# Two transformer blocks on one core: seven of eight rows of four norms squared and summed one stage earlier, and the mixers' first weights asked for first

## What is computed

```python
def rms_norm(x, g):
    xf = x.astype(jnp.float32)
    y = xf * lax.rsqrt(jnp.mean(xf * xf, axis=-1, keepdims=True) + EPS)
    return (y * g.astype(jnp.float32)).astype(x.dtype)
...
        h = h + 0.5 * swiglu(rms_norm(h, g_ffn1[i]), w_ffn1_gate[i], w_ffn1_up[i], w_ffn1_down[i])
        u = rms_norm(h, g_mix[i]) @ w_in[i]
...
        h = h + jnp.concatenate([o_mla, o_diff], axis=-1) @ w_out[i]
        h = h + 0.5 * swiglu(rms_norm(h, g_ffn2[i]), w_ffn2_gate[i], w_ffn2_up[i], w_ffn2_down[i])
        gate = jax.nn.sigmoid(rms_norm(h, g_ple_in[i]) @ w_ple_gate[i] + b_ple_gate[i])
        h = h + gate * rms_norm(p[i] @ w_ple_proj[i], g_ple_out[i])
...
        h = h + mixer(rmsnorm(h, norm_mix_g[l]), w_in[l], ...)
```

## Time and profile before

| | |
|---|---|
| median of 3 runs | 2608.38 us (2603.45 to 2608.44) |
| the profiled execution | 2611.73 us |
| its span in the trace | 2609.8 us |
| TensorE busy | 2296.4 us, 88% |
| VectorE busy | 961.0 us, 37% |
| ScalarE busy | 451.7 us, 17% |
| GpSimd busy | 50.8 us, 2% |
| granted TensorE clock, mean | 0.94 |

### The profile page before, as it was taken

One profiled execution on the slowest core, in us unless ns is written; L12 is line 12 of the kernel. 1 busy time (PEld: TensorE's weight loads), 2 busy tenths in 40 slices (PEclk: granted clock), 3 DMA queues, 4 the chain that ended last, 5 costly groups with the idle time before them and its releaser, 6 DMA issues.

```text
span 2609.8 us, 26212 instructions
## 1 busy us (share of the span) xinstructions
PE 2296.4 (88%) x10107; PEld 1560.8 (60%) x10107; DVE 961.0 (37%) x1961; ACT 451.7 (17%) x851; POOL 50.8 (2%) x76
## 2 busy tenths in 40 slices
PE   7999999989989999999989997779999587777783
PEld 5888887336644888887558774456785332222231
DVE  5454433133743455434310207876651300000003
ACT  2000001253351001000210014432113000000001
POOL 0000000000000000000000000000000000000001
PEclk9999999999999999999989987789999699989997
DMA  3232222111005323231132210000332589999996
GB/s 128 65 97 87 87 88 91 46 35 33 1 9 181 118 79 97 75 119 57 41 90 69 65 41 1 1 9 1 97 113 92 226 372 429 428 430 429 429 415 246
DMA packets 172359, 359.92 MB, mean 138 GB/s; under 512 B 15665, under 2 KB 144305, under 8 KB 155874
## 3 DMA queue, kind: packets, MB, share of 16 engines
q1 hardware_dynamic: 163744, 326.89, 33.8%
q0 software_dynamic: 5600, 21.10, 2.1%
q10 hardware_dynamic: 2914, 10.56, 1.0%
HBM read 337.49 MB, written 21.04 MB: 137 GB/s over the span
## 4 chain that ended last, share of the span: by engine, by line
PE 27%; DMA 12%; DVE 5%; issue 4%; DVEq 2%; ACT 1%; POOLq 1%; SPq 1%; POOL 0%; ACTq 0%
DMA M<-w 12%; PE PS L2905 7%; PE PS L69 6%; PE PS L2289 5%; PE PS L2471 2%; PE PS L1563 1%; DVE M L1880 1%; DVEq L1884 1%; PE PS L2044 1%; DVE M L1874 1%; PE PS L1573 1%; PE PS L1986 0%; POOLq L258 0%; DVE M L1896 0%; PE PS L1800 0%
## 5 line engine op out<-in xcount | busy, mean ns | idle before, releaser
L575 PE MATMUL PS<-M 128*128 128x256 f32 x2464 | 542.4, 382 | 12.5 <-DVE M L324 7.3
L575 PEld LDWEIGHTS PS<-M 128*128 128x128 f32 x2464 | 469.2, 191 | 86.6 <-DMA M<-w_ffn_up 13.2
L2905 PE MATMUL PS<-M 128*64 128x512 f32 x1536 | 370.3, 640 | 97.4 <-DMA M<-w 93.1
L2905 PEld LDWEIGHTS PS<-M 128*64 128x64 f32 x1536 | 122.6, 147 | 333.6 <-issue 279.6
L606 PE MATMUL PS<-M 128*128 128x256 f32 x1232 | 268.6, 379 | 4.8 <-DVE M L690 2.5
L606 PEld LDWEIGHTS PS<-M 128*128 128x128 f32 x1232 | 233.4, 190 | 41.7 <-issue 10.3
L69 PE MATMUL PS<-M 128*128 128x264 f32 (+1 forms) x824 | 208.5, 416 | 23.0 <-ACT M L313 9.6
L69 PEld LDWEIGHTS PS<-M 128*128 128x128 f32 x824 | 160.0, 196 | 71.0 <-issue 23.2
L2975 DVE TENSOR_TENSOR M<-M,PS 128x512 f32<-128x512 f32 x16 | 11.0, 687 | 434.3 <-PE PS L2905 434.3
L693 DVE TENSOR_TENSOR M<-M,PS 128x256 f32<-128x256 f32 x220 | 92.6, 421 | 201.1 <-PE PS L575 197.0
L2289 PE MATMUL PS<-M 128*128 128x264 f32 x616 | 142.8, 394 | 8.1 <-DVE M L2388 5.1
(11 more groups left out here) (365 smaller groups left out, 2263.5 us busy)
## 6 DMA issues: line engine op xcount, KB each, us to landing
M<-w SPq DMA_DIRECT2D x64, 2048.0 KB, 21.2
M<-w SPq DMA_DIRECT2D x64, 1024.0 KB, 21.9
M<-w_ffn_gate SPq DMA_DIRECT2D x22, 1024.0 KB, 5.4
M<-w_ffn_up SPq DMA_DIRECT2D x22, 1024.0 KB, 5.4
M<-w_ffn_down SPq DMA_DIRECT2D x16, 1024.0 KB, 5.1
M<-w_in SPq DMA_DIRECT2D x13, 1024.0 KB, 5.3
M<-w_in SPq DMA_DIRECT2D x25, 512.0 KB, 3.8
expert_rows<-M POOLq DMA_DIRECT2D x2, 4096.0 KB, 24.4
```

Of the source, the lines that this page charges most:

```text
L575: last = nc.tensor.matmul(PS[:, 3 * half + BANK[p], 0:HALF], lhs[:, a, :], rhs[:, a, :], start=p in FIRST and a == 0, stop=p in LAST and a ...
L2905: last = nc.tensor.matmul(PS[ROWS * k:ROWS * k + ROWS, bank, :], wide[:, a * P + ROWS * k:a * P + ROWS * k + ROWS], weights(k), start=star ...
```

## The change

Four of the five norms are split: those of the first mixer, the second FFN, the gate, and the second mixer. Rows 0 to 6 are squared by ScalarE in the stage before, each when it is final (`norm_front_act`; in the gate stage `squared` between the sigmoids), after the table for Ln has been loaded (in the gate stage the table is loaded after the squares). The squares go to their own place: `xnT` after an FFN, `WORK0` in the w_out stage, `WORK0 + 20000` in the gate stage. GpSimd adds rows 1 to 5 to row 0, one at a time with a drain between (`norm_front_pool`). At the end of the stage, still ahead of the barrier, TensorE multiplies the folded row and row 6 by the ones (`norm_front_pe`). After the barrier ScalarE squares row 7 alone, TensorE adds it, and Ln follows.

In the first mixer SP asks for the two first blocks of `w_in` ahead of the three tables. In the second it asks for the two first blocks ahead of the wait for `zeroed` and the eleven small loads. The loop over the gate's sigmoids and the one over the first eight weight blocks are unrolled.

```diff
@@
+        FOLDED = KD - 2
+        def norm_front_act(act, src, squares, ready, lo=0):
+            for a in range(lo, KD - 1):
+                ready(a)
+                nc.scalar.activation(squares[:, a, :], src[:, a, :], ACT.Square).then_inc(sq_ready, 1)
+
+        def norm_front_pool(pool, squares):
+            base = count("pool", sq_ready)
+            after("pool", sq_ready, KD)
+            for a in range(1, FOLDED):
+                pool.wait_ge(sq_ready, base + a + 1)
+                last = nc.gpsimd.tensor_tensor(squares[:, 0, :], squares[:, 0, :], squares[:, a, :], ALU.add)
+                if a == FOLDED - 1:
+                    last.then_inc(rows_folded, 1)
+                else:
+                    pool.drain()
+
+        def norm_front_pe(pe, G, squares):
+            pe.wait_ge(sq_ready, count("pe", sq_ready) + KD - 1)
+            pe.wait_ge(rows_folded, after("pe", rows_folded))
+            G.matmul(nc, PS, 6, ones, squares[:, 0, :], True, False)
+            G.matmul(nc, PS, 6, ones, squares[:, KD - 2, :], False, False)
+
+        def norm_pe(pe, G, squares=None):
+            if squares is not None:
+                pe.wait_ge(sq_ready, after("pe", sq_ready, KD))
+                G.matmul(nc, PS, 6, ones, squares[:, KD - 1, :], False, True).then_inc(ss_ready, 1)
+                return
             for a in range(KD):
...
-        def norm_act(act, G, src):
...
+        def norm_act(act, G, src, squares=None):
+            if squares is None:
...
+            else:
+                nc.scalar.activation(squares[:, KD - 1, :], src[:, KD - 1, :], ACT.Square).then_inc(sq_ready, 1)
             act.wait_ge(ss_ready, after("act", ss_ready))
...
+        SQ_FFN = xnT[:, :, 0:S1]
+        SQ_OUT = at(WORK0, KD, S1)
+        SQ_PLE = at(WORK0 + 20000, KD, S2)
@@ ffn_pe, at its end
+            norm_front_pe(pe, G1, SQ_FFN)
@@ ffn_act, at its end
+            nc.scalar.preload_act_table_set(LN)
+            norm_front_act(act, h1, SQ_FFN,
+                           lambda a: act.wait_ge(d_taken, 9 * (rnd * DPAIRS + a // 2) + DOWN_TAKES["P4" if a % 2 else "P3"]))
@@ proj1_sp
-            sp.dma_start(WQ, I["w_q_up"].rearrange("(a p) n -> p a n", p=P)).then_inc(wqkv_in, 16)
-            sp.dma_start(WKV, I["w_kv_up"]).then_inc(wqkv_in, 16)
-            sp.dma_start(dist, I["c_dist"]).then_inc(tables_in, 16)
             w_in = I["w_in"].rearrange("(a p) n -> p a n", p=P)
             for lo, cols in ((0, 256), (256, 160)):
...
+            sp.dma_start(WQ, I["w_q_up"].rearrange("(a p) n -> p a n", p=P)).then_inc(wqkv_in, 16)
+            sp.dma_start(WKV, I["w_kv_up"]).then_inc(wqkv_in, 16)
+            sp.dma_start(dist, I["c_dist"]).then_inc(tables_in, 16)
@@ mix1_pe, mix1_act
+            residual_pe(pe, KD, lambda a: mixT[:, a, 0:S1]); norm_front_pe(pe, G1, SQ_OUT); stage(pe, "pe")
...
+            rings["act"].loop_over(KD // 2)
+            nc.scalar.preload_act_table_set(LN)
+            rows = after("act", acc_free, KD) - KD
+            norm_front_act(act, h1, SQ_OUT, lambda a: act.wait_ge(acc_free, 2 + rows + a + 1)); stage(act, "act")
@@ ple_pe, ple_act
+            residual_pe(pe, KD, lambda a: xnT[:, a, 0:S1], row_ready=tiles)
+            norm_front_pe(pe, G2, SQ_PLE); stage(pe, "pe")
...
+            def squared(n):
+                act.wait_ge(acc_free, 2 + rows + n + 1)
+                nc.scalar.activation(SQ_PLE[:, n, :], hT[:, n, :], ACT.Square).then_inc(sq_ready, 1)
+
+            for n in range(KD):
+                s, ready, use = ring.chunk()
+                act.wait_ge(w_used[s], use + 1)
+                act.wait_ge(pgate_free, n + 1)
+                nc.scalar.activation(pgate[:, n % 2, :], PS[:, 4 + n % 2, :], ACT.Sigmoid,
+                                     bias=g["b_ple_gate"][:, n:n + 1]).then_inc(pgate_ready, 1)
+                if n > 0:
+                    squared(n - 1)
+            nc.scalar.preload_act_table_set(LN)
@@ proj2_sp
+            def head_weights(c):
+                s, ready, use = ring.chunk()
+                sp.wait_ge(w_used[s], use)
+                sp.dma_start(slot(s, 0, KD, P), w2cols(OFF["ka" if c % 2 else "qa"] + c // 2 * P, P)).then_inc(w_ready[s], 16)
+
+            for c in range(2):
+                head_weights(c)
             sp.wait_ge(zeroed, 1)
...
-            for lo0, lo1 in ((OFF["qa"], OFF["ka"]), (OFF["qb"], OFF["qi"])):
...
+            for c in range(2, 8):
+                head_weights(c)
...
@@ the engines' programs
+                norm_front_pool(pool, SQ_FFN); stage(pool, "pool")
...
-                norm_pe(pe, G1); ffn_pe(pe); stage(pe, "pe")
+                norm_pe(pe, G1, SQ_OUT); ffn_pe(pe); stage(pe, "pe")
```

More of the change, by code:

```diff
@@ L309, in norm_pe @@
             last.then_inc(ss_ready, 1)
-        def norm_act(act, G, src):
-            for a in range(KD):
-                nc.scalar.activation(xnT[:, a, 0:G.T], src[:, a, :], ACT.Square).then_inc(sq_ready, 1)
-            nc.scalar.preload_act_table_set(LN)
+        def norm_act(act, G, src, squares=None):
+            if squares is None:
+                for a in range(KD):
+                    nc.scalar.activation(xnT[:, a, 0:G.T], src[:, a, :], ACT.Square).then_inc(sq_ready, 1)
+                nc.scalar.preload_act_table_set(LN)
+            else:
+                nc.scalar.activation(squares[:, KD - 1, :], src[:, KD - 1, :], ACT.Square).then_inc(sq_ready, 1)
             act.wait_ge(ss_ready, after("act", ss_ready))
@@ L1400, in ple_pe @@
         def ple_pe(pe):
-            norm_pe(pe, G1)
+            norm_pe(pe, G1, SQ_FFN)
             tiles = count("pe", xn_ready)
             after("pe", xn_ready, KD)
-            residual_pe(pe, KD, lambda a: xnT[:, a, 0:S1], row_ready=tiles); stage(pe, "pe")
+            residual_pe(pe, KD, lambda a: xnT[:, a, 0:S1], row_ready=tiles)
+            norm_front_pe(pe, G2, SQ_PLE); stage(pe, "pe")
         def ple_act(act):
             ring = rings["act"]
-            norm_act(act, G1, h1)
+            norm_act(act, G1, h1, SQ_FFN)
             nc.scalar.preload_act_table_set(SIGMOID)
-            with act.Fori(0, KD // 2) as i:
-                for k in range(2):
-                    s, ready, use = ring.looped(i, k)
-                    act.wait_ge(w_used[s], use + 1)
-                    act.wait_ge(pgate_free, i * 2 + (k + 1))
-                    nc.scalar.activation(pgate[:, k:k + 1, :], PS[:, 4 + k:5 + k, :], ACT.Sigmoid,
-                                         bias=g["b_ple_gate"][:, ds(i * 2 + k, 1)]).then_inc(pgate_ready, 1)
-            ring.loop_over(KD // 2)
+            rows = after("act", acc_free, KD) - KD
+            def squared(n):
[9 more added lines that the diff above has]
+                    squared(n - 1)
+            nc.scalar.preload_act_table_set(LN)
             stage(act, "act")
@@ L1437, in ple_pool @@
         def ple_pool(pool):
-            stage(pool, "pool")
+            norm_front_pool(pool, SQ_PLE); stage(pool, "pool")
         cos2, sin2 = at(WORK0, S2), at(WORK0 + 528, S2)
@@ L1486, in proj2_sp @@
                          I["w_uv_2"].rearrange("h c d -> c h d")).then_inc(small_in, 16)
-            for lo0, lo1 in ((OFF["qa"], OFF["ka"]), (OFF["qb"], OFF["qi"])):
-                with sp.Fori(0, 4) as i:
-                    for k in range(2):
-                        s, ready, use = ring.looped(i, k)
-                        sp.wait_ge(w_used[s], use)
-                        sp.dma_start(slot(s, 0, KD, P), W2[:, :, ds(i * P + (lo0, lo1)[k], P)]).then_inc(w_ready[s], 16)
-                ring.loop_over(4)
+            for c in range(2, 8):
+                head_weights(c)
+            with sp.Fori(0, 4) as i:
+                for k in range(2):
+                    s, ready, use = ring.looped(i, k)
+                    sp.wait_ge(w_used[s], use)
+                    sp.dma_start(slot(s, 0, KD, P), W2[:, :, ds(i * P + (OFF["qb"], OFF["qi"])[k], P)]).then_inc(w_ready[s], 16)
+            ring.loop_over(4)
             for c in range(2):
@@ L2590, in mix2_pe @@
         def mix2_pe(pe):
-            norm_pe(pe, G2); proj2_pe(pe); stage(pe, "pe")
+            norm_pe(pe, G2, SQ_PLE); proj2_pe(pe); stage(pe, "pe")
             stick_pe(pe); early_gate_pe(pe)
@@ L3076, in _ @@
             stage(pool, "pool")
-            if stop > 1: stage(pool, "pool")
+            after("pool", sq_ready, KD)
+            if stop > 1:
+                norm_front_pool(pool, SQ_FFN); stage(pool, "pool")
             if stop > 2: mix1_pool(pool)
             if stop > 3:
-                zero_rows_pool(pool); stage(pool, "pool")
+                zero_rows_pool(pool)
+                norm_front_pool(pool, SQ_FFN); stage(pool, "pool")
             if stop > 4: ple_pool(pool)
@@ L3105, in _ @@
             if stop > 3:
-                norm_act(act, G1, h1); ffn_act(act); stage(act, "act")
+                norm_act(act, G1, h1, SQ_OUT); ffn_act(act); stage(act, "act")
             if stop > 4: ple_act(act)
```

13 lines of the change are left out of this document (6 added, 7 removed).

## The result

The changed kernel takes 2584.63 us (median of 4 runs, 2580.78 to 2588.16) against 2608.41 for the kernel before: a ratio of 0.9918, with a 95% interval of 0.9891 to 0.9944. Six more runs (e1) gave 2585.54 and again 0.9918 (0.9904 to 0.9933). So the gain is 21 us by the ratio, 17 to 25 by the narrower interval; 20.0 were forecast.

The account below looks back on a forecast made before the run. Four stage boundaries were the target, TensorE's sums slower than ScalarE's squares; VectorE's weight sums nearly level before the second FFN. 4.9 + 0.2 + 4.9 + 10.0 = 20.0 us: profiled 2611.73 to 2591.7, median 2588.4; 80% range 2582 to 2599.

Parts of the forecast that it names:

- TensorE's sums are the price of a boundary: First FFN to first mixer: TensorE, not ScalarE, is the slower partner; sums take 7.1 us, the eight squares 4.3.
- A and C: Boundaries first FFN to first mixer (A) and second FFN to per-layer gate (C): fewer sums gain 4.9 us each.
- The first mixer's load: First w_in load: in the old order a new 2.5 us wait; asked for first, hidden with 1.9 us to spare.
- B: Boundary from w_out to second FFN: VectorE's weight sums still hold it, so only 0.2 us gained.
- D: Boundary from gate to second mixer: fewer sums and no wait for weights, less a barrier shift, gain 10.0 us.
- The third block behind the small loads: Second mixer: the third w_in block lands in time, 1.2 us to spare in the worst case; taken at nothing.
- rival 2: Second mixer's third block late behind the small loads, its boundary gives nothing: gain 10 us, 2598; chance 0.06.
- GpSimd: Row adds ahead of the four barriers: 27 us in all, none on the path; 2 us for the high end.
- rival 3: GpSimd's adds lock out VectorE's weight sums while TensorE waits: 27 us against 20 gained, 2615; chance 0.03.
- The clock at the restarts: TensorE's lower clock after each restart: taken at nothing, with ends of -2.5 to +1.6 us kept.
- Rival 1: Clock takes back half: a second low stretch at four restarts returns 11 us, gain 9, 2599; chance 0.09.
- a sign of being wrong: Stages between the boundaries: the forecast is wrong if they grow; no size given.

Follow-up runs that it names:

- e1: The changed kernel run again unaltered, for a narrower interval and a second trace; median 2585.54 us, ratio 0.9918 to the kernel before.
- e4: The changed kernel without GpSimd's adds, TensorE summing rows 0 to 6 itself ahead of the barrier; median 2608.93 us, ratio 1.000 to the kernel before.
- e2: The changed kernel with the first mixer's loads in their old order, w_in after the three tables; median 2590.67 us, ratio 0.9934 to the kernel before.
- e6: The changed kernel with the second FFN's second-block weight sums moved behind the norm; median 2583.69 us, ratio 0.9911 to the kernel before.
- e5: The changed kernel with the second FFN's norm unsplit, as it was before; median 2588.67 us, ratio 0.9928 to the kernel before.
- e3: The changed kernel with the second mixer's first two blocks behind the eleven small loads again; median 2600.41 us, ratio 0.9974 to the kernel before.
- e9: The kernel before, unaltered, run again for a second trace; the second mixer's stretch from last projections to gates took 304.0 us.
- e8: The changed kernel with one Ln-and-Exp table everywhere, second-block weight sums behind the second FFN's norm, and an earlier folded-row product before the second mixer; 2562.50 us, output 6% off.
- e7: The changed kernel with the table holding both Ln and Exp wherever the Ln table was loaded; median 2563.51 us, ratio 0.9825, output 6% off.
- e12: e11's kernel with the table holding both Ln and Exp at the five row norms alone; median 2582.21 us, ratio 0.9894 to the kernel before.
- e11: The changed kernel with second-block weight sums behind the second FFN's norm and the folded-row product ahead of row 6's square before the second mixer; 2583.29 us, ratio 0.9897.

## Why the prediction was right, point by point

**TensorE's sums are the price of a boundary, not ScalarE's squares.** Right, and e4 shows it: with the squares early and the sums still on TensorE, A and C gain 0.4 us of 4.7, and nothing is left of the gain in time.

**A and C, 4.9 each; measured 4.68 and 4.67.** Barrier to first product was put at 5.5 and is 5.59 (445.34 - 439.75). The barrier was put 1.8 us behind the last product and is 1.92 behind it: the four early instructions take 1.98 us with their drain.

**The first mixer's load.** Forecast 2.5 us if the order had stayed; e2 shows 2.25, and the release by the DMA. Asked for first it was to land after 5.4 us with 1.9 to spare; it landed after 5.3 with 2.2.

**B, 0.2 us; measured 0.44 and 0.16 (e1).** The reason given, VectorE's weight sums from the landing of w_ffn_gate, is shown by e6, where moving half of them takes off 2.7 us, and by e5.

**D, 10.0; measured 10.48.** From the barrier to the first product 5.6 was forecast and 5.66 measured. The step that was off is the barrier's shift: I took 1.1 us, and it is 0.6 (3.41 us behind the last product against 2.79). Row 6's square follows the sigmoid at once, and the eight instructions take 2.05 us. What I called two parts, 7.9 us of sums and 3.2 us of waiting for weights, don't add as they were added: without the reordering nothing of it comes by way of the sums (e3), and with the reordering but the sums still on TensorE it is 6.0 us (e4). The total was right since both edits were made. That the sum over the four boundaries is within 0.3 us of 20.0 owes something to luck: A and C fell short by 0.2 each, and D came out 0.5 over.

**The third block behind the small loads** is asked for when TensorE has used the first (1335.71), not when SP is free (1332.84). No wait; rival 2 didn't come. The prediction gives its cover once as 1.2 us in the worst case and once, in rival 2, as 4; it was 3.6.

**GpSimd.** Its adds came in time everywhere; at D the last ends at 1313.65, 5.4 us ahead of TensorE's early sums. Their price on VectorE was put too low, 0.36 us where a row add lost 0.82 and the scaling ahead of C 4.1 in all, and none of it was on the path, so that rival 3 didn't come either.

**The clock at the restarts** was taken at nothing. In the first trace of after it rises 3.8, 3.8, 4.6 and 2.9 us behind the first product at A to D, where it had been 4.4, 5.5, 3.5 and 5.6. Windows after the restarts at A and D in the first trace of after:

```profile
445.30:449.10 3.80, 3.76 (x5) 1.65 (x6) 3.80 (x7) 0.00 (x0) 0.00 (x0) 0.56 1.03 404
...
1326.80:1329.80 3.00, 2.93 (x7) 2.35 (x8) 3.00 (x5) 0.00 (x0) 0.00 (x0) 0.50 1.14 204
```

At A the first moments are still at the full clock in both. The time at the lower level behind the four restarts is 17.9 us before and 14.8 after in the first pair of traces, but 15.1 (e9) and 18.6 (e1) in the second: half of the difference, 1.6 us gained and 1.8 lost. So nothing was a fair value for it. Rival 1, which had half the gain lost to it, didn't come.

**What the sum left out.** It treated all between the boundaries as fixed. In the first pair of traces 10.6 of the 30.9 us between the spans lie outside the boundaries: 2.4 ahead of the first FFN and 1.5 inside it, 1.3 in the second mixer's projections and 4.8 in the stretch hold most of it. In the second pair (e9 and e1) it is 8.0 of 28.2, and the stretch alone holds 8.3. Two stages grew, which the prediction named as a sign of being wrong: the first mixer by 1.5 and 1.8 us in the two pairs (368.8 to 370.3, 368.0 to 369.8), the gate stage by 0.6 and 0.5, where the clock rises 1.1 and 1.0 us later behind C. The first mixer's growth is open.

The median came within 4 us of the forecast all the same. The boundaries give 20.3 and 20.2 us in the two pairs. Were the stretch's 4.8 or 8.3 us typical too, the gain would be 25 or 28 us, at the end of the interval (17 to 25) or over it. So most of that is in the traces alone, and how much of the 21 us is the stretch's stays open. Also open is what e3 and e4 lose beyond their boundaries in a typical run.

## What to carry to other kernels

Before moving work ahead of a barrier, see which engine of the pair sets the pace: squares that were made early were worth 0.4 us of 4.7 at A and C while TensorE still summed them one by one, and folding them on an idle engine was the gain. A shorter chain uncovers what ran beside it, here the first weight load at A and VectorE's weight sums at B (at D the load was the limit already), so work out the landing time of each load against the new start and move it in the same change. Compare traces boundary by boundary; a difference of spans mixes in stages that nobody touched.

## What the runs showed of the hardware beyond what was expected

A chain of short steps at a clock that keeps going up and down has no fixed length: the same 1360 TensorE instructions took 295.6 to 304.1 us over these traces, sorted by where the clock first fell in them. Edits hundreds of microseconds earlier went with one end or the other: 303.9 and 304.1 in two traces of e4's kernel, 295.9 and 295.7 in two of the changed one, though 300.7 and 304.0 in two of the kernel before. Edits that took 3.7 and 3.9 us off the boundaries lost 3.5 of them there in their traces (e8 against e7, e12 against e11). A GpSimd add of 1.3 to 1.4 us stretched a VectorE add with two SBUF inputs from 0.69 to 1.51 us.
